# The conformer's LayerNorm placed inside the in-projection of a two-layer hybrid trunk

## The chip, the cores and the metric

One core of a Trainium2 chip runs the whole program. The metric is device time in microseconds (us) from one launch; lower is better. The core's engines work from queues of their own and meet through semaphores: TensorE (PE, with its weight loads PEld), VectorE (DVE), ScalarE (ACT), GpSimd (POOL) and SyncE (SP), which issues the loads.

## The reference, cut to what matters

Two layers, 512 tokens, width 1024, everything float32. In each layer one projection of the normed input feeds four mixers: A, a gated short convolution; B, a conformer convolution; C, a blockwise causal attention (MoBA, four heads of 64); D, a latent attention (MLA, four heads) whose query and key/value latents are normed by RMS. Their outputs are joined, projected, normed and added; a convolutional FFN follows. The change concerns mixer B:

```python
def conformer_conv_mixer(z, w_conv, b_conv, ln_g, ln_b):
    a, g = jnp.split(z, 2, axis=-1)
    u = a * jax.nn.sigmoid(g)
    u = causal_dwconv(u, w_conv) + b_conv.astype(u.dtype)
    return jax.nn.silu(layernorm(u, ln_g, ln_b))
```

`layernorm` takes the mean over the 256 channels of a token, subtracts it, divides by the root of the mean square (plus 1e-6), and applies a gain and a bias.

## The kernel before, in words

Activations lie transposed: channels on the 128 partitions, 512 tokens along the free axis. Every float32 product is made of three reduced-precision ones (`product`, lines 500 to 503): each operand is split in a high part, rounded by ScalarE ("hi"), and a low part, the rest, made by VectorE ("lo"); hi x hi, hi x lo and lo x hi are summed in one PSUM bank. Weights go the same way: SP loads a unit into `raw`, ScalarE writes its high part (line 400, `split_hi`), VectorE its low part (line 408, `split_lo`), in a ring of four.

The order of work is written out by hand, engine by engine. The in-projection is 21 groups, `for g in range(4, G_MK)` and `first_groups` on TensorE; a group is 24 products of 512 columns. Groups 0 to 3 feed the conformer, 4 to 9 MoBA, 10 to 14 the MLA latents (10 the key/value latent "ckv", 12 to 14 the query latents "cq"), 15 to 20 the gated convolution (gate, product, value; two halves). VectorE and ScalarE run the same loop `for g in range(G_MK)` with their work for each group. The conformer's 31 taps are spread over groups 3 to 14: one half of the channels is summed by VectorE in PSUM bank 7 (`CF_BANK`, lines 1074 and 1079), the other by ScalarE and POOL (lines 1373 and 824); both end in `cf_out`.

A norm over channels crosses partitions, so TensorE does it. There are three such events per layer, "ckv", "cq" and "ln", and each goes: ScalarE squares (`square`, line 1308, into `sq`), POOL adds the squares (`sums`, line 806), TensorE sums over partitions with a column of ones (`stat`, line 607, eight fp32 instructions into bank 4, `STAT`), VectorE makes the variance (`event_var`, line 952), POOL raises it to -1/2 (`rsqrt`, line 810, `rstd`), TensorE spreads it over the partitions (`spread`, line 614, eight fp32 instructions, again into `STAT`), VectorE multiplies. The LayerNorm also needs its mean, two fp32 products with a matrix of ones (line 659).

Before the change TensorE has: ckv's column sums after group 13, its spreading after group 15; cq's after 17 and 18; the LayerNorm's mean after group 19, into `STAT`; then the latent projections (keys `G_MK`, values `G_MV`, rope queries `G_MR`, queries `G_MQ`), with the LayerNorm's column sums between the two query groups; then the attention loop. POOL runs ckv, cq, the LayerNorm's sum, the rotation of the rope queries (lines 833 and 835), and then the LayerNorm's power.

The attention loop has 32 steps, one for a head (four MoBA, four MLA) and a chunk of 128 queries, with keys growing 128 to 512. A step: TensorE's `scores`; VectorE's masking and row maximum (line 1122) and, a step later, the reciprocal of the row sum (line 1130); ScalarE's exponential (line 1440); POOL's scaling (line 841, `prob`); three steps later TensorE's `transposes` (line 722), a head's four chunks taking one to four of them; ScalarE's high part (line 1432) and VectorE's low part (line 1136) of the transposed probabilities; then `values`. At step 2 POOL also makes the low part of the rope queries (line 845). The LayerNorm's second half hangs in these steps: TensorE's spreading at step 2, VectorE's products at 2 (line 1141), 5 and 6 (line 1146), 9 and 10 (line 1152), ScalarE's gain and tanh at 3 and 4 (lines 1445 and 1448) and high part at 6 and 7 (line 1452).

Banks are handed on through `bank_taken_over` and `bank_free`: a group waits until the last reader of its bank is done; so the second query group waits for the second gate's value product (line 1064), and the rope queries wait for the low parts of the three query latents (line 1085).

## Time and profile before

| | |
|---|---|
| three runs | 1259.45, 1260.35, 1263.19 us (median 1260.35) |
| the profiled execution | 1256.69 us, of it the span from first to last instruction 1254.6 us |
| TensorE busy | 1211.7 us, 97% of the span |
| VectorE, ScalarE, POOL busy | 820.4, 581.2, 208.8 us |
| mean granted clock of TensorE | 0.978 of full |

TensorE's busy time is modelled from pipelined instructions, and an instruction's duration reaches into the next one's start; so steps on TensorE are best read from start to start. The granted clock is 1.00 at 2.4 GHz and 0.50 at 1.2 GHz. A wait is put down to the semaphore that came last. The in-projection of layer 0 ends near 146 us of the span, its attention near 223.

### The profile page before, as it was taken

How to read it: one execution, taken by the hardware profiler on the slowest of the kernel's cores; microseconds unless marked ns; L12 is line 12 of the kernel's file. 1: busy time of each engine (PE TensorE's matmuls, PEld its weight loads, DVE VectorE, ACT ScalarE, POOL GpSimd, SP SyncE). 2: the span in 40 equal slices, each digit the busy share in tenths (PEclk: the TensorE clock that was granted, in tenths of full speed). 3: DMA queues.
4: the chain of work that ended last, by engine and by line, in shares of the span. 5: the costliest groups of instructions: out<-in, count | busy, mean ns of one | idle time of the engine just before them, and what ended most of it. 6: DMA issues, size and time to landing. Idle time of an engine off the chain costs nothing.

```text
span 1254.6 us, 15488 instructions
## 1 busy us (share of the span) xinstructions
PE 1211.7 (97%) x6006; PEld 1020.4 (81%) x6006; DVE 820.4 (65%) x1160; ACT 581.2 (46%) x879; POOL 208.8 (17%) x190
## 2 busy tenths in 40 slices
PE   6999999999999999999999999999999999999996
PEld 6887878888888888888888877788888888888885
DVE  4699557487666666544758976766766666664463
ACT  4455357454444344434545634755444444443432
POOL 1285136020000000000005822531000000000000
PEclk9999968999999999999999998899999999999998
DMA  8232312442333333466633333135233333336573
GB/s 241 80 85 82 88 43 84 148 138 85 101 101 101 96 90 100 146 190 216 202 85 98 84 94 86 33 133 169 85 113 90 100 101 91 94 101 199 171 231 121
DMA packets 157083, 147.36 MB, mean 117 GB/s; under 512 B 6831, under 2 KB 137811, under 8 KB 157011
## 3 DMA queue, kind: packets, MB, share of 16 engines
q1 hardware_dynamic: 156432, 145.64, 38.8%
q8 instruction: 48, 0.79, 0.3%
q10 hardware_dynamic: 579, 0.74, 0.2%
q14 instruction: 24, 0.20, 0.1%
HBM read 140.07 MB, written 2.10 MB: 113 GB/s over the span
## 4 chain that ended last, share of the span: by engine, by line
PE 82%; DVE 12%; POOL 2%; issue 2%; ACT 1%; DMA 1%; POOLq 0%; DVEq 0%; ACTq 0%
PE ps L501 26%; PE ps L503 26%; PE ps L502 26%; DVE ps L1074 3%; DVE wsp L408 3%; PE ps L722 2%; DVE rot L971 1%; PE ps L563 1%; POOL prob L841 1%; DVE shuf L969 1%; POOL rms_r L815 1%; DVE hid L976 1%; DVE xn L915 1%; DMA rows<-in_vectors 1%; POOL wsp L408 1%
## 5 line engine op out<-in xcount | busy, mean ns | idle before, releaser
L501 PE MATMUL ps<-xn,wsp 128*128 128x512 f32 (+2 forms) x1136 | 418.8, 369 | 11.4 <-DVE xn L915 11.4
L502 PE MATMUL ps<-xn,wsp 128*128 128x512 f32 (+2 forms) x1136 | 416.1, 366 | 0.0
L503 PE MATMUL ps<-xn,wsp 128*128 128x512 f32 (+2 forms) x1136 | 416.0, 366 | 0.0
L408 DVE TENSOR_TENSOR wsp<-raw,wsp 128x1024 fp32r<-128x1024 f32 (+1 forms) x250 | 311.1, 1247 | 155.5 <-ACT wsp L400 155.3
L400 ACT ACTIVATE wsp<-raw 128x1024 fp32r<-128x1024 f32 (+1 forms) x256 | 266.8, 1043 | 177.6 <-PE ps L503 146.5
L501 PEld LDWEIGHTS ps<-xn,wsp 128*128 128x128 f32 (+1 forms) x1136 | 215.1, 189 | 48.3 <-DVE xn L915 13.6
L502 PEld LDWEIGHTS ps<-xn,wsp 128*128 128x128 f32 (+1 forms) x1136 | 215.2, 189 | 35.0 <-issue 0.5
L503 PEld LDWEIGHTS ps<-xn,wsp 128*128 128x128 f32 (+1 forms) x1136 | 215.1, 189 | 34.9
L501 PE MATMUL ps<-wsp,hid 128*128 128x512 f32 (+1 forms) x488 | 189.7, 389 | 0.0
L503 PE MATMUL ps<-wsp,hid 128*128 128x512 f32 (+1 forms) x488 | 189.1, 388 | 0.0
L502 PE MATMUL ps<-wsp,hid 128*128 128x512 f32 (+1 forms) x488 | 189.0, 387 | 0.0
L815 POOL TENSOR_TENSOR rms_r<-rms_v,power 128x1 f32<-128x1 f32 x32 | 29.1, 913 | 833.9 <-DVE rms_v L880 833.9
L503 PEld LDWEIGHTS ps<-wsp,hid 128*128 128x128 f32 x488 | 91.6, 188 | 18.8
L502 PEld LDWEIGHTS ps<-wsp,hid 128*128 128x128 f32 x488 | 91.7, 188 | 18.6
L501 PEld LDWEIGHTS ps<-wsp,hid 128*128 128x128 f32 x488 | 91.7, 188 | 18.5
L824 POOL TENSOR_TENSOR cf_out<-cf_out,cf_tmp 128x512 f32<-128x512 f32 x60 | 94.4, 1573 | 71.1 <-ACT cf_tmp L1373 64.2
L1203 DVE SCALAR_TENSOR_TENSOR c_v<-ps,vec_all,c_v 128x511 f32<-128x511 f32 x44 | 33.0, 749 | 86.7 <-ACT c_v L1496 86.7
L1496 ACT ACTIVATE c_v<-ps,vec_all 128x512 f32<-128x512 f32 x44 | 30.3, 688 | 100.5 <-PE ps L503 100.5
L1203 DVE SCALAR_TENSOR_TENSOR c_g<-ps,vec_all,c_g 128x511 f32<-128x511 f32 x44 | 33.0, 750 | 62.7 <-ACT c_g L1496 62.7
L1496 ACT ACTIVATE c_g<-ps,vec_all 128x512 f32<-128x512 f32 x44 | 30.3, 688 | 76.6 <-PE ps L503 76.6
L1501 ACT ACTIVATE hid<-c_v 128x512 fp32r<-128x512 f32 x44 | 27.9, 633 | 62.0 <-DVE c_v L1225 62.0
L841 POOL TENSOR_TENSOR prob<-prob,rowinv 128x128 f32<-128x128 f32 (+1 forms) x64 | 45.6, 720 | 55.6 <-DVE rowinv L1130 55.4
(138 smaller groups left out, 1319.8 us busy)
## 6 DMA issues: line engine op xcount, KB each, us to landing
raw<-in_w_ffn_up SPq DMA_DIRECT2D x88, 512.0 KB, 3.8
raw<-in_w_ffn_down SPq DMA_DIRECT2D x88, 512.0 KB, 4.2
raw<-in_w_in SPq DMA_DIRECT2D x40, 512.0 KB, 3.9
raw<-in_w_out SPq DMA_DIRECT2D x32, 512.0 KB, 3.9
x<-in_x SPq DMA_DIRECT2D x4, 512.0 KB, 8.4
xn<-xn SPq DMA_DIRECT2D x8, 256.0 KB, 3.2
out_x<-x SPq DMA_DIRECT2D x4, 512.0 KB, 4.2
xn<-kr SPq DMA_DIRECT2D x8, 128.0 KB, 3.0
```

Source lines behind the costliest of these rows:

```text
L400: act.activation(wsp[:, u % SPLIT, 0, 0:nk * n], raw[:, r, 0:nk * n], ACT.Copy).then_inc(hi_done, 1)
L408: eng.tensor_tensor(wsp[:, u % SPLIT, 1, 0:nk * n], raw[:, (l * NU + u) % RAW, 0:nk * n], fp(wsp[:, u % SPLIT, 0, 0:nk * n]), ALU.subtract ...
L501: pe.matmul(dst, a[0], b[0], start=start, stop=False, skip_group_check=True)
L502: pe.matmul(dst, a[0], b[1], start=False, stop=False, skip_group_check=True)
L503: return pe.matmul(dst, a[1], b[0], start=False, stop=stop, skip_group_check=True)
L815: pool.tensor_tensor(rms_r[:, i:i + 1], rms_v[:, i:i + 1], power[:, 0:1], ALU.pow).then_inc(rms_rstd, 1)
L824: pool.tensor_tensor(cf_out[:, 1, :], cf_out[:, 1, :], cf_tmp[:, j % 2, :], ALU.add)\
L841: pool.tensor_tensor(prob[:, t % NPROB, 0:n], prob[:, t % NPROB, 0:n], rowinv[:, t:t + 1].to_broadcast([P, n]), ALU.mult).then_inc(prob_do ...
L1074: st.mark(dve.scalar_tensor_tensor(ps[:, CF_BANK, :], cf_u[:, 0, j:j + T], col(l, "conv_b", 2 * j), ps[:, CF_BANK, :], ALU.mult, ALU.add))
L1203: st.mark(dve.scalar_tensor_tensor(cc[:, 1:T], ps[:, bank, 0:T - 1], col(l, "conv_ffn", 2 * NF + half * NF + p), cc[:, 1:T], ALU.mult, ALU ...
L1496: act.activation((c_v if half else c_g)[:, :], ps[:, bank_of(G_UP + j), :], ACT.Copy, scale=col(l, "conv_ffn", 4 * NF + half * NF + p)).th ...
L1501: act.activation(hid[:, p, 0, :], c_v[:, :], ACT.Copy).then_inc(f_hi, 1)
```

## The change

The LayerNorm moves ahead as a whole. Its mean goes behind group 16, into bank 7, where VectorE's running sum of the taps has just ended, instead of bank 4; its column sums stand in the middle of group 18 and its spreading behind cq's after group 18, both in bank 7. It gets tiles of its own (`ln_sq`, `ln_var`, `ln_rstd`), so that it can run beside cq. ckv's spreading goes from after group 15 to after group 16, and VectorE's use of it from group 16 to 17. VectorE and ScalarE do the rest of the LayerNorm, with its gain, tanh and splitting, in groups 17 to 20; nothing of it is left in the attention steps. VectorE makes the low parts of the query latents in group 20, ahead of the second gate's value product, instead of after it. POOL's order becomes: power of ckv, sums of cq, sum of ln, power of cq, power of ln. The second value group, which uses bank 7, now waits for `cf_norm`. The scratch `sq`/`sm` moves by 96 bytes.

The diff, without the new tiles and the moves of those few bytes:

```diff
@@ -237,6 +240,10 @@
         ps = ctx.enter_context(nc.psum_tensor("ps", [P, 8, T], f32))
+        EV_BANK = dict(ckv=STAT, cq=STAT, ln=CF_BANK)
+        EV_SQ = dict(ckv=sq, cq=sq, ln=ln_sq)
+        EV_VAR = dict(ckv=var, cq=var, ln=ln_var)
+        EV_RSTD = dict(ckv=rstd, cq=rstd, ln=ln_rstd)
@@ -508,10 +515,10 @@
-def dense(u, bank, rhs, m=P, c0=0, cols=slice(0, T)):
+def dense(u, bank, rhs, m=P, c0=0, cols=slice(0, T), ks=None):
     w = weights(u)
     nk = len(rhs)
-    for k in range(nk):
+    for k in ks or range(nk):
         last = product(ps[0:m, bank, cols], (w[:, 0, k, c0:c0 + m], w[:, 1, k, c0:c0 + m]), rhs[k],
@@ -604,14 +611,14 @@
     for c in range(TC):
-        last = pe.matmul(ps[:, STAT, c:c + 1], sq[:, 0, c * P:(c + 1) * P], ones[:, 0:1],
+        last = pe.matmul(ps[:, EV_BANK[ev], c:c + 1], EV_SQ[ev][:, 0, c * P:(c + 1) * P], ones[:, 0:1],
                          start=True, stop=True)
...
     for c in range(TC):
-        last = pe.matmul(ps[:, STAT, c * P:(c + 1) * P], rstd[:, c:c + 1].to_broadcast([P, P]),
+        last = pe.matmul(ps[:, EV_BANK[ev], c * P:(c + 1) * P], EV_RSTD[ev][:, c:c + 1].to_broadcast([P, P]),
                          ident[:, :], start=True, stop=True)
@@ -641,23 +648,27 @@
             weights_ready(l, g)
-            last = dense(g, bank_of(g), x_pairs, m=MLA_QK if g == G_KR else P)
+            if g == 18:
+                dense(g, bank_of(g), x_pairs, ks=range(KD // 2))
+                stat("ln", l)
+                last = dense(g, bank_of(g), x_pairs, ks=range(KD // 2, KD))
+            else:
+                last = dense(g, bank_of(g), x_pairs, m=MLA_QK if g == G_KR else P)
         last.then_inc(group_done, 1)
...
             stat("ckv", l)
-        if g == 15:
+        if g == 16:
             spread("ckv", l)
+            pe.wait_ge(cf_conv, l + 1)
+            pe.wait_ge(cf_sum, (l + 1) * (CF_TAPS - 1))
+            for c in range(2):
+                last = pe.matmul(ps[:, CF_BANK, :], ones[:, :], cf_out[:, c, :], start=c == 0, stop=c == 1)
+            last.then_inc(mean_done, 1)
         if g == 17:
...
             spread("cq", l)
-        if g == 19:
-            pe.wait_ge(cf_conv, l + 1)
-            pe.wait_ge(cf_sum, (l + 1) * (CF_TAPS - 1))
-            pe.wait_ge(lat_norm, l * 4 + 4)
-            for c in range(2):
-                last = pe.matmul(ps[:, STAT, :], ones[:, :], cf_out[:, c, :], start=c == 0, stop=c == 1)
-            last.then_inc(mean_done, 1)
+            spread("ln", l)
@@ -669,6 +680,8 @@
         bank_taken_over(l, g)
+        if bank_of(g) == CF_BANK:
+            pe.wait_ge(cf_norm, l * 2 + 2)
         for j in range(2):
@@ -685,8 +698,6 @@
         dense(U_UQ, bank_of(g), latents, c0=i * P).then_inc(group_done, 1)
-        if i == 0:
-            stat("ln", l)
@@ -746,8 +757,6 @@
             scores(t)
-        if t == 2:
-            spread("ln", l)
         if TRAIL <= t < N_ATT + TRAIL:
@@ -756,7 +765,6 @@
     pe.wait_ge(y_ready, l * 4 + 4)
-    pe.wait_ge(cf_norm, l * 2 + 2)
     pe.wait_ge(masked, (l + 1) * N_ATT)
@@ -803,11 +811,12 @@
             pool.wait_ge(add_done, l * NADD + adds_before(ev) + k - 1)
-        pool.tensor_tensor(sq[:, 0, :], sq[:, 0, :], sq[:, 1, :], ALU.add).then_inc(add_done, 1)
+        tile = EV_SQ[ev]
+        pool.tensor_tensor(tile[:, 0, :], tile[:, 0, :], tile[:, 1, :], ALU.add).then_inc(add_done, 1)
...
     pool.wait_ge(var_done, l * NEV + EVENTS.index(ev) + 1)
-    pool.tensor_tensor(rstd[:, :], var[:, :], power[:, :], ALU.pow).then_inc(rstd_done, 1)
+    pool.tensor_tensor(EV_RSTD[ev][:, :], EV_VAR[ev][:, :], power[:, :], ALU.pow).then_inc(rstd_done, 1)
@@ -823,17 +832,17 @@
             .then_inc(cf_sum, 1)
-    for ev in ("ckv", "cq"):
-        sums(ev, l)
-        rsqrt(ev, l)
+    rsqrt("ckv", l)
+    sums("cq", l)
     sums("ln", l)
+    rsqrt("cq", l)
+    rsqrt("ln", l)
...
     pool.tensor_tensor(ml_rot[:, :], ml_rot[:, :], ml_shuf[:, :], ALU.add).then_inc(rot_done, 1)
-    rsqrt("ln", l)
@@ -949,7 +958,7 @@
     dve.wait_ge(stat_done, l * NEV + EVENTS.index(ev) + 1)
-    dve.tensor_scalar(var[:, :], ps[:, STAT, 0:TC], 1.0 / WIDTH[ev], EPS, ALU.mult, ALU.add)\
+    dve.tensor_scalar(EV_VAR[ev][:, :], ps[:, EV_BANK[ev], 0:TC], 1.0 / WIDTH[ev], EPS, ALU.mult, ALU.add)\
        .then_inc(var_done, 1)
@@ -976,7 +985,7 @@
     def group_a_lo(c):
-        dve.wait_ge(y_hi, l * 4 + c + 1)
+        dve.wait_ge(y_hi, l * 4 + 3 * c + 1)
         dst = hid[:, Y_SLOT["a"] + c]
@@ -999,7 +1008,7 @@
             event_var("ckv" if g == 14 else "cq", l)
-        if g == 16:
+        if g == 17:
             scale_ready("ckv", l)
@@ -1007,18 +1016,39 @@
                                      ALU.mult, ALU.subtract).then_inc(lat_ready, 1)
+        if g == 17:
+            dve.wait_ge(mean_done, l + 1)
+            for c in range(2):
+                dve.scalar_tensor_tensor(cf_out[:, c, :], ps[:, CF_BANK, :], -1.0 / GW, cf_out[:, c, :],
+                                         ALU.mult, ALU.add).then_inc(cf_cent, 1)
         if g == 18:
             group_a_lo(0)
+            event_var("ln", l)
         if g == 19:
...
                    .then_inc(lat_norm, 1)
+        if g == 19:
+            scale_ready("ln", l)
+            for c in range(2):
+                dve.tensor_tensor(cf_out[:, c, :], cf_out[:, c, :], ps[:, CF_BANK, :], ALU.mult)\
+                   .then_inc(cf_norm, 1)
+            for c in range(2):
+                dve.wait_ge(cf_swish, l * 2 + c + 1)
+                dve.scalar_tensor_tensor(cf_out[:, c, :], cf_th[:, c, :], 1.0, cf_out[:, c, :],
+                                         ALU.add, ALU.mult).then_inc(cf_val, 1)
         if g == 20:
-            dve.wait_ge(mean_done, l + 1)
+            for j in range(3):
+                dve.wait_ge(lat_hi, l * 4 + j + 2)
+                dst = hid[:, CQN + j]
+                dve.scalar_tensor_tensor(dst[:, 1, :], lat[:, j, :], col(l, "mla_q_norm", j),
+                                         fp(dst[:, 0, :]), ALU.mult, ALU.subtract).then_inc(lat_ready, 1)
             for c in range(2):
-                dve.scalar_tensor_tensor(cf_out[:, c, :], ps[:, STAT, :], -1.0 / GW, cf_out[:, c, :],
-                                         ALU.mult, ALU.add).then_inc(cf_cent, 1)
+                dve.wait_ge(y_hi, l * 4 + c + 2)
+                dst = hid[:, Y_SLOT["b"] + c]
+                dve.scalar_tensor_tensor(dst[:, 1, :], cf_out[:, c, :], 0.5, fp(dst[:, 0, :]),
+                                         ALU.mult, ALU.subtract).then_inc(y_ready, 1)
         if g in (1, 3):
@@ -1079,18 +1109,13 @@
     own(sc_val, l * 2 + 2)
-    for j in range(3):
-        dve.wait_ge(lat_hi, l * 4 + j + 2)
-        dst = hid[:, CQN + j]
-        dve.scalar_tensor_tensor(dst[:, 1, :], lat[:, j, :], col(l, "mla_q_norm", j),
-                                 fp(dst[:, 0, :]), ALU.mult, ALU.subtract).then_inc(lat_ready, 1)
     group_a_lo(1)
...
                           ALU.subtract).then_inc(kn_ready, 1)
-    own(y_ready, l * 4 + 2)
+    own(y_ready, l * 4 + 4)
     for half in range(2):
@@ -1105,8 +1130,6 @@
                           ALU.subtract).then_inc(qn_ready, 1)
-        if i == 0:
-            event_var("ln", l)
@@ -1135,22 +1158,6 @@
                .then_inc(pt_ready, 1)
-        if t == 2:
-            scale_ready("ln", l)
-            for c in range(2):
-                dve.tensor_tensor(cf_out[:, c, :], cf_out[:, c, :], ps[:, STAT, :], ALU.mult)\
-                   .then_inc(cf_norm, 1)
-        if t in (5, 6):
-            c = t - 5
-            dve.wait_ge(cf_swish, l * 2 + c + 1)
-            dve.scalar_tensor_tensor(cf_out[:, c, :], cf_th[:, c, :], 1.0, cf_out[:, c, :],
-                                     ALU.add, ALU.mult).then_inc(cf_val, 1)
-        if t in (9, 10):
-            c = t - 9
-            dve.wait_ge(y_hi, l * 4 + c + 3)
-            dst = hid[:, Y_SLOT["b"] + c]
-            dve.scalar_tensor_tensor(dst[:, 1, :], cf_out[:, c, :], 0.5, fp(dst[:, 0, :]),
-                                     ALU.mult, ALU.subtract).then_inc(y_ready, 1)
         h, r = divmod(t - TRAIL - VALUES_AFTER[2] - 2, TC)
@@ -1301,11 +1308,11 @@
     if k == 0:
-        if l or EVENTS.index(ev):
+        if ev != "ln" and (l or EVENTS.index(ev)):
             act.wait_ge(stat_done, l * NEV + EVENTS.index(ev))
...
         act.wait_ge(add_done, l * NADD + adds_before(ev) + k - 1)
-    act.activation(sq[:, min(k, 1), :], src, ACT.Square).then_inc(sq_done, 1)
+    act.activation(EV_SQ[ev][:, min(k, 1), :], src, ACT.Square).then_inc(sq_done, 1)
@@ -1391,28 +1398,39 @@
         if g == 17:
+            for c in range(2):
+                act.wait_ge(cf_cent, l * 2 + c + 1)
+                square("ln", c, cf_out[:, c, :], l)
             group_a_hi(0)
+        if g == 19:
+            for c in range(2):
+                act.wait_ge(cf_norm, l * 2 + c + 1)
+                act.activation(cf_out[:, c, :], cf_out[:, c, :], ACT.Identity,
+                               scale=col(l, "ln_b_gain", c), bias=col(l, "ln_b_bias", c))\
+                   .then_inc(cf_affine, 1)
+                act.wait_ge(cf_affine, l * 2 + c + 1)
+                act.activation(cf_th[:, c, :], cf_out[:, c, :], ACT.Tanh, scale=0.5).then_inc(cf_swish, 1)
         if g == 20:
...
                                scale=col(l, "mla_q_norm", j)).then_inc(lat_hi, 1)
+            for c in range(2):
+                act.wait_ge(cf_val, l * 2 + c + 1)
+                act.activation(hid[:, Y_SLOT["b"] + c, 0, :], cf_out[:, c, :], ACT.Copy, scale=0.5)\
+                   .then_inc(y_hi, 1)
         if g >= G_SC and (g - G_SC) % 3 == 0:
...
             act.activation(sc_w[:, :], ps[:, bank_of(g), :], ACT.Copy).then_inc(sc_gate, 1)
-        if g == 20:
-            for c in range(2):
-                act.wait_ge(cf_cent, l * 2 + c + 1)
-                square("ln", c, cf_out[:, c, :], l)
     group_a_hi(1)
...
         act.activation(ml_k[2 * i][:, 0, :], ps[:, bank_of(G_MK + i), :], ACT.Copy).then_inc(kn_hi, 1)
-    act.wait_ge(y_ready, l * 4 + 2)
+    act.wait_ge(y_ready, l * 4 + 4)
     for half in range(2):
@@ -1439,18 +1457,6 @@
                            scale=-1.0, accum_out=rowsum[:, t:t + 1]).then_inc(exp_done, 1)
-        if t in (3, 4):
-            c = t - 3
-            act.wait_ge(cf_norm, l * 2 + c + 1)
-            act.activation(cf_out[:, c, :], cf_out[:, c, :], ACT.Identity, scale=col(l, "ln_b_gain", c),
-                           bias=col(l, "ln_b_bias", c)).then_inc(cf_affine, 1)
-            act.wait_ge(cf_affine, l * 2 + c + 1)
-            act.activation(cf_th[:, c, :], cf_out[:, c, :], ACT.Tanh, scale=0.5).then_inc(cf_swish, 1)
-        if t in (6, 7):
-            c = t - 6
-            act.wait_ge(cf_val, l * 2 + c + 1)
-            act.activation(hid[:, Y_SLOT["b"] + c, 0, :], cf_out[:, c, :], ACT.Copy, scale=0.5)\
-               .then_inc(y_hi, 1)
         if t == 1:
...
         if t in (12, 16, 20):
```

## Rows read from the trace of the kernel before

**Rows 1.** The page: busy time, and the granted clock in 40 slices

```profile
PE 1211.7 (97%) x6006; PEld 1020.4 (81%) x6006; DVE 820.4 (65%) x1160; ACT 581.2 (46%) x879; POOL 208.8 (17%) x190
...
PEclk9999968999999999999999998899999999999998
```

**Rows 2.** Waits of TensorE: us in total, times, longest us

```profile
PE ps L614 <- POOL rstd L810: 3.0, 2, 1.5
```

**Rows 3.** Windows: us, busy of PE, PEld, DVE, ACT, POOL, clock, DMA share, GB/s

```profile
165.46:196.18 30.72, 30.72 (x118) 25.43 (x117) 16.30 (x55) 17.43 (x47) 10.32 (x13) 0.50 0.07 17
776.45:793.52 17.07, 17.07 (x60) 12.77 (x60) 9.48 (x34) 10.80 (x29) 7.11 (x10) 0.50 0.35 76
```

**Rows 4.** Timeline of TensorE after group 15: start us, us, what, idle before

```profile
114.23 1.16 PE L614 MATMUL ps<-ident,rstd 128*128 128x128 f32 x8 [1.48 <-POOL rstd L810]
```

**Rows 5.** Timeline of TensorE after groups 18 and 19, layer 0

```profile
132.52 1.05 PE L614 MATMUL ps<-ident,rstd 128*128 128x128 f32 x8
133.33 0.48 PE L501 MATMUL ps<-xn,wsp 128*128 128x512 f32 x1
...
138.89 1.88 PE L659 MATMUL ps<-cf_out,ones 128*128 128x512 f32 x4
```

**Rows 6.** Timeline of TensorE at the start of the rope queries, layer 0

```profile
148.64 0.28 PE L502 MATMUL ps<-wsp,hid 128*128 128x256 f32 x1
148.76 0.28 PE L503 MATMUL ps<-wsp,hid 128*128 128x256 f32 x1
149.15 0.50 PE L501 MATMUL ps<-hid,wsp 128*128 128x512 f32 x1
```

**Rows 7.** Timeline of TensorE at the entry into attention, layer 0

```profile
156.43 0.33 PE L501 MATMUL ps<-hid 64*128 64x128 f32 x1
...
158.12 0.44 PE L501 MATMUL ps<-hid 64*128 64x384 f32 x1 [0.74 <-DVE negmax L1122]
...
158.84 1.16 PE L614 MATMUL ps<-ident,rstd 128*128 128x128 f32 x8
159.92 0.49 PE L501 MATMUL ps<-hid 64*128 64x512 f32 x1
...
165.20 0.91 PE L722 MATMUL ps<-ident,prob 128*128 128x128 f32 x4 [0.98 <-POOL prob L841]
```

**Rows 8.** Timeline of TensorE at the entry into attention, layer 1

```profile
776.23 1.91 PE L614 MATMUL ps<-ident,rstd 128*128 128x128 f32 x8
778.07 0.79 PE L501 MATMUL ps<-hid 64*128 64x512 f32 x1
...
784.53 1.11 PE L722 MATMUL ps<-ident,prob 128*128 128x128 f32 x4
```

**Rows 9.** Timeline of TensorE, groups of four transposes of later heads, both layers

```profile
196.70 0.60 PE L722 MATMUL ps<-ident,prob 128*128 128x128 f32 x4
...
794.74 0.66 PE L722 MATMUL ps<-ident,prob 128*128 128x128 f32 x4
...
806.71 0.60 PE L722 MATMUL ps<-ident,prob 128*128 128x128 f32 x4
```

**Rows 10.** Timeline of POOL: the LayerNorm's sum and power, attention steps 2, 3

```profile
144.68 1.29 POOL L806 TENSOR_TENSOR sq<-sq 128x512 f32<-128x512 f32 x1 [14.12 <-ACT sq L1308]
...
156.08 1.02 POOL L810 TENSOR_TENSOR rstd<-var,power 128x4 f32<-128x4 f32 x1
...
162.86 1.28 POOL L845 TENSOR_TENSOR ml_rope<-ml_rot,ml_rope 128x512 fp32r<-128x512 f32 x1
164.09 1.06 POOL L841 TENSOR_TENSOR prob<-prob,rowinv 128x512 f32<-128x512 f32 x1
```

**Rows 11.** Timeline of VectorE: last tap, second gate, low parts of the query latents

```profile
114.56 0.75 DVE L1079 SCALAR_TENSOR_TENSOR cf_out<-cf_u,vec_all,ps 128x512 f32<-128x512 f32 x1
...
139.08 0.69 DVE L1052 TENSOR_TENSOR sc_u<-ps,sc_w 128x512 f32<-128x512 f32 x1 [2.91 <-PE ps L503]
...
147.01 2.08 DVE L1085 SCALAR_TENSOR_TENSOR hid<-lat,vec_all,hid 128x512 fp32r<-128x512 f32 x3
```

More of the change, by code:

```diff
@@ L182, in hybrid_trunk_kernel @@
         rstd = place("rstd", [P, TC], f32)
+        ln_var = place("ln_var", [P, TC], f32)
+        ln_rstd = place("ln_rstd", [P, TC], f32)
         power = place("power", [P, TC], f32)
@@ L193, in hybrid_trunk_kernel @@
         sc_u = place("sc_u", [P, T + 2], f32, tmp_at + 4096)
-        sq = place("sq", [P, 2, T], f32, tmp_at + 10336)
-        sm = place("sm", [P, 2, T], f32, tmp_at + 10336)
+        sq = place("sq", [P, 2, T], f32, tmp_at + 10240)
+        sm = place("sm", [P, 2, T], f32, tmp_at + 10240)
         prob = place("prob", [P, NPROB, T], f32, tmp_at + 4096)
@@ L202, in hybrid_trunk_kernel @@
         junk = place("junk", [P, D], bf16, tmp_at + 12288, width=2)
-        assert tmp_at + 14432 <= nc.sbuf_usable_end, (tmp_at + 14432, nc.sbuf_usable_end)
+        assert tmp_at + 14336 <= nc.sbuf_usable_end, (tmp_at + 14336, nc.sbuf_usable_end)
         Y_SLOT = dict(a=0, b=2, c=4, d=6)
@@ L229, in hybrid_trunk_kernel @@
         ml_shuf = place("ml_shuf", [P, T], f32, slot(Y_SLOT["d"]) + 4 * T)
+        ln_sq = place("ln_sq", [P, 2, T], f32, slot(Y_SLOT["d"] + 1))
         ml_rope = place("ml_rope", [P, 2, T], f32r, slot(Y_SLOT["d"] + 1))
```

## The prediction

> **What bounds the kernel now.** I read the page first: TensorE is busy 97% of the span [rows 1], so what counts is its work, its idle time and its clock; another engine matters only where TensorE waits for it. The list of TensorE's waits then says which of them this change can reach [rows 2]: 3.0 us, twice 1.5, behind POOL's rsqrt `rstd` at line 810 (the ckv norm of each layer). The rest of what it can reach is read from the timelines around its places. The clock is the third thing. The windows give its two low stretches [rows 3]: 30.72 us in layer 0 and 17.07 us in layer 1 at 0.50 (1.2 GHz), and the page's clock line shows every other slice up to the last at nine tenths or more (1.00, 2.4 GHz) [rows 1]. Both begin a few us after attention begins and end inside it.
>
> The cost of the low level is read from the groups of four transposes that close a head's steps [rows 7 to 9]. In layer 0 three heads, from 165.20 to 196.70, took 31.50 us; in layer 1 two heads at the full level, from 794.74 to 806.71, took 11.97, which is 5.99 a head. So layer 0 lost about 31.50 - 3 x 5.99 = 13.5 us, and layer 1 in its one slow head (784.53 to 794.74, 10.21 us) 4.2 us and a little before that.
>
> **The change, part by part.** Most of what moves costs TensorE the same wherever it stands: the eight column sums of `stat("ln")` and the four products of the mean keep their kind and count. What differs:
>
> 1. *The ckv spreading goes from after group 15 to after group 16.* Its `rstd` came 1.48 us after TensorE was ready [rows 4]; now a whole group of 24 products lies between, and DVE's last tap of the running sum, which the mean waits for, ends at 115.3 [rows 11], also before group 16 can end. The wait goes: -1.48 per layer, -2.96.
>
> 2. *The wait before the rope queries goes.* `dense(U_UR)` started 0.39 us after the product ahead of it [rows 6], where products of that shape follow at 0.12, because the three low parts of the q latents were made at 147.01 for 2.08 us [rows 11], behind the second gate's product. They now stand ahead of that product. The wait goes: -0.27 per layer, -0.54. Late next is the second gate itself, which the second query group's bank waits for. DVE had 2.91 us idle ahead of group 19's gate [rows 11]; it now puts four LayerNorm operations there, whose two last ones follow ScalarE's tanh. Counted on, the gate's product ends some 3 us before TensorE asks for its bank: cost 0, or up to +1 per layer if ScalarE's turns are slower.
>
> 3. *The ln spreading is now behind the cq spreading, between groups 18 and 19.* Eight fp32 products took 0.81 us there, 132.52 to 133.33 [rows 5]: +0.81 per layer, +1.62. Its `rstd` has the second half of group 18, the column sums and the cq spreading as cover. POOL's power itself takes 1.02 [rows 10], with the variance on DVE ahead of it. If that cover failed it would cost up to +1 per layer; I take 0.
>
> 4. *The column sums in the middle of group 18* wait for POOL's sum of squares. From the mean's start, 138.89 [rows 5], to the end of that sum, 144.68 + 1.29 [rows 10], it took 7.1 us. Now the mean, group 17, the cq sums and half of group 18 lie between, by the same spacing about 10.5 us. Cost 0, with 3 us to spare. On POOL the sum now stands ahead of `rsqrt("cq")`, which is wanted only after group 18.
>
> 5. *The entry into attention.* In layer 0 the first score started at 156.43 and the first four transposes at 165.20 [rows 7], 8.77 us. The 0.74 us wait for the first mask stays: it hangs on the second query group's low part, which nothing here brings nearer. The spreading's 1.08 us (158.84 to 159.92) goes, and with it the two LayerNorm products on DVE that held back the fourth mask. But the fourth `prob` also stood behind POOL's rope subtraction [rows 10], which stays. Replaying the chain, the four transposes come about 1.2 us earlier, with a wait of about 0.9 still ahead of them. That holds if the clock stays up so long. If it falls at the fourth score, the entry takes what layer 1's took from there, 784.53 - 778.07 = 6.46 us [rows 8], and comes at 8.96 us: +0.2. I take the middle, -0.5. In layer 1 the spreading itself ran at the low level, 776.23 to 778.07 [rows 8]: 1.84 us go and the rest is as before, -1.74 after 0.1 for the restart. If the clock there holds longer, up to -3.1.
>
> 6. *DVE's and ScalarE's LayerNorm operations in steps 2 to 10 go.* TensorE was busy throughout the low stretches [rows 3], so that relief buys nothing there: 0.
>
> Sum: -2.96 - 0.54 + 1.62 - 0.5 - 1.74 = **-4.1 us**. The profiled execution took 1256.69 us (span 1254.6), so it would take 1252.6. But the three runs shown stand at 1259.45 to 1263.19, their median 1260.35 lying 3.66 above the profiled one. I read that as low stretches of other lengths, an estimate: layer 1's alone would have lost 9 us more had it lasted as long as layer 0's. I take the sum off the median: **1256.2 us**.
>
> **Where a rule and the rows part.** Before both falls TensorE did short scores, transposes and waits of at most 0.98 us [rows 7]; in layer 1 the fall came at 776.45, within the eight spreading products [rows 3, 8], in layer 0 only 6.6 us after they had begun. So the plain products of the spreading did not keep the clock up in layer 1 and may have delayed the fall in layer 0; that is the choice made in step 5. The Trainium skill, "TensorE: Matmul & The Clock Gate", section "Part 4: PE-mode transpose", says that transposes do not count as a busy TensorE in the way other products do. By that rule the change speaks against itself, since it takes eight plain products out of a stretch that holds transposes; layer 0's entry would then be the +0.2 of step 5 and the sum -3.4.
>
> **The rivals.**
>
> *The gain is eaten by a longer low stretch.* For it: layer 0 shows that the stretch can last until the MLA heads, layer 1 that it can end two heads sooner, and nothing in the change sets which. If layer 1's lasts like layer 0's it loses 13.5 - 4.2 = 9.3 us more than in the profile: 1252.6 + 9.3 = 1261.9. With only one more slow head in either layer, 4.5 us: 1257.1 on the profile's base, 1259 to 1260 on the median's. Against it: the runs shown probably hold such stretches already. Chance 0.24, result 1257 to 1262, no change.
>
> *The clock does not fall in one layer.* For it: the entry is shorter by a spreading. Against it: the 0.74 us wait, the half-height scores and the POOL wait all stay, and TensorE has less work between them. It would save 4 to 13.5 us more: about 1247. Chance 0.08.
>
> *DVE becomes the bound around groups 19 to 21.* For it: seven operations more there, about 5 us with the turns to ScalarE, and the second gate, the key and value low parts and the first mask queue behind them on DVE. It decides once DVE ends its chain later than ScalarE ends the second query group's high part; from there each us on DVE is one us of TensorE, in both layers. Against it: DVE's idle stretches there [rows 11]. One us late in both gives 1256.2 + 2 = 1258.2. Chance 0.10.
>
> *Slower: the low level reaches into the MLA heads.* There the full level held in both layers once it had come back [rows 1, 3]. If the shifted schedule makes it stay low through the four MLA heads of one layer, that is 4 x (10.5 - 5.99) = 18 us (10.5 is a third of layer 0's 31.50): 1256.2 + 18 = 1274; a single such head, with the longer stretch above, 1265. Against it: the rise in layer 0 came just there, at 196.18. It decides where the low stretch outlasts the first MLA head, within which it ended in layer 0. Chance 0.08.
>
> *The change doesn't do what it says.* It does: every instruction of `ln` leaves the attention loop; no chance of its own.
>
> **How the numbers follow.** The forecast has 0.50; its own range is 1253.5 to 1258.5, from step 5's ends and the +1 of steps 2 and 3. Steps of 0.3% (3.8 us, about what a measurement of this kernel can tell from no change) stand at 1256.6 and 1264.1. The forecast is so near the first that about 0.42 of its 0.50 lies below it. Faster: 0.42 + 0.08 = 0.50. Same: 0.08 + 0.24 + 0.10 = 0.42. Slower: 0.08. The range for 8 in 10 leaves out the slower case, and the better part of the missing fall: 1250.5 to 1262.
>
> **What would show it.** In the changed profile: the wait of TensorE on `rstd` gone from the list of waits; the three latents' wait gone; two spreadings back to back after group 18; the first score of layer 0 about 0.9 us earlier; the four transposes 7.5 to 9 us after it; the fourth `prob` still waiting behind the rope subtraction; two low stretches of the clock, each beginning in the entry. Wrong would be: a TensorE wait in the middle of group 18 or ahead of group 19, a first mask later than 1.35 us after the first score, or low stretches whose total differs from 47.8 us by so much that the 4 us drown in it.

## The result: 8.7 us faster, 3.3 us below the range

| | before | after |
|---|---|---|
| median of the runs compared | 1255.92 us (20 runs, 1246.69 to 1263.19) | 1247.20 us (20 runs, from 1244.45) |
| ratio | | 0.995, 95% interval 0.9927 to 0.9973 |
| profiled execution, its span | 1256.69, 1254.6 us | 1257.87, 1256.1 us |

The prediction said 1256.2 us (1250.5 to 1262.0). The 8.7 us are the difference of the medians; by the means of the same runs (1254.8 and 1249.0) it is 5.8. One disturbed execution of the changed kernel, 6798.82 us, takes no part in the ratio. Two things stand out. The kernel before, with 17 more runs, has a median of 1255.92, not the 1260.35 of the three runs shown ahead of the prediction. And the profiled execution of the changed kernel was one of its longest, so its total misleads; it has to be read stage by stage.

The page of the changed kernel, busy time and granted clock:

```profile
PE 1217.1 (97%) x6006; PEld 1026.6 (82%) x6006; DVE 822.8 (66%) x1160; ACT 581.7 (46%) x879; POOL 208.7 (17%) x190
...
PEclk9999959999999999999999998699999999999999
```

The instruction counts are those of [rows 1]: nothing was added or left out. From the list of TensorE's waits (us in total, times, longest us), the two that stand in the attention's entry and heads:

```profile
PE ps L733 <- POOL prob L850: 3.6, 8, 0.6
PE ps L508 <- DVE negmax L1145: 1.5, 2, 0.7
```

The 3.0 us behind `rstd` [rows 2] are gone; the wait for the first mask stayed, twice 0.7. TensorE's timeline of layer 0: the two spreadings after group 18, the start of the rope queries, the first and third score, the first transposes, the first group of four. After the dots, the first score and the first group of four of layer 1.

```profile
132.53 1.05 PE L621 MATMUL ps<-ident,rstd 128*128 128x128 f32 x8
133.42 1.06 PE L621 MATMUL ps<-ident,ln_rstd 128*128 128x128 f32 x8
...
147.90 0.28 PE L510 MATMUL ps<-wsp,hid 128*128 128x256 f32 x1
148.02 0.40 PE L508 MATMUL ps<-hid,wsp 128*128 128x512 f32 x1
...
154.26 0.32 PE L508 MATMUL ps<-hid 64*128 64x128 f32 x1
...
155.95 0.44 PE L508 MATMUL ps<-hid 64*128 64x384 f32 x1 [0.73 <-DVE negmax L1145]
...
157.37 0.33 PE L733 MATMUL ps<-ident,prob 128*128 128x128 f32 x1
...
161.56 1.12 PE L733 MATMUL ps<-ident,prob 128*128 128x128 f32 x4
...
769.59 0.32 PE L508 MATMUL ps<-hid 64*128 64x128 f32 x1
...
777.08 1.11 PE L733 MATMUL ps<-ident,prob 128*128 128x128 f32 x4
```

The first score of layer 1 in the kernel before:

```profile
773.83 0.33 PE L501 MATMUL ps<-hid 64*128 64x128 f32 x1
```

The rope queries start 0.12 us after the product ahead of them, where it was 0.39 [rows 6]. From the first score to the first four transposes it is 7.30 us, where it was 8.77 [rows 7], and the 0.98 us wait ahead of them is gone too. In layer 1 it is 7.49 us (769.59 to 777.08), where it was 10.70 (773.83 to the 784.53 of [rows 8]). What hides this in the total is the clock. The windows of its low stretches, layers 0 and 1 (columns as in [rows 3]):

```profile
159.39:193.52 34.13, 34.04 (x126) 27.91 (x127) 15.15 (x55) 16.45 (x46) 13.21 (x16) 0.50 0.11 23
773.79:807.92 34.13, 34.13 (x128) 27.59 (x126) 15.40 (x59) 17.16 (x47) 13.02 (x16) 0.50 0.13 28
```

In layer 1 the stretch was twice as long as in [rows 3], and it ran, as there, with TensorE busy all through.

Stage by stage, all from starts in TensorE's timeline (us). The 80 transposes of an attention are counted here in fours, in the order in which they are issued: "first", "third", "fourth" and "fifth" are the starts of numbers 1, 9, 13 and 17. These fours are not the groups of four that close a head: the first head's group is numbers 7 to 10, the second head's begins with number 17.

| stage | before, layers 0 / 1 | after, layers 0 / 1 |
|---|---|---|
| program start to ckv's column sums, layer 0 | 100.76 | 99.73 |
| ckv's column sums to the first score | 55.68 / 55.71 | 54.53 / 54.54 |
| first score to first | 4.38 / 5.81 | 3.11 / 3.10 |
| first to fourth | 9.47 / 10.17 | 9.50 / 9.68 |
| fourth to the last transposes | 48.97 / 40.03 | 49.30 / 48.76 |

From the column sums to the fourth the change gained 2.39 us in layer 0 and 4.37 in layer 1, **6.76 us** in all (7.00 up to the first head's group of four, the mark that the prediction used), where the prediction's sum had 4.1. The longer low stretch took 8.73 back in the last row of layer 1. The first row differs by 1.03 us for work that the change does not touch; in a second profile of the changed kernel it was 100.76 again.

### The profile page after: what moved, and what is told of

It reads as the page before. It is cut to its first block, busy times and chain, and to the rows that moved or that the text cites. A ratio compares the mean times of both kernels' runs of the same rounds, so it can differ in the third digit from the quotient of the medians.

```text
span 1256.1 us, 15486 instructions
## 1 busy us (share of the span) xinstructions
PE 1217.1 (97%) x6006; PEld 1026.6 (82%) x6006; DVE 822.8 (66%) x1160; ACT 581.7 (46%) x879; POOL 208.7 (17%) x190
## 4 chain that ended last, share of the span: by engine, by line
PE 88%; DVE 4%; POOL 4%; issue 1%; ACT 1%; DMA 1%; POOLq 0%; DVEq 0%; ACTq 0%
PE ps L508 28%; PE ps L510 28%; PE ps L509 28%; PE ps L733 2%; POOL cf_out L833 2%; POOL rms_r L824 1%; POOL prob L850 1%; PE ps L570 1%; DVE xn L924 1%; DMA rows<-in_vectors 1%; DVE wsp L415 1%; DVE yt L904 1%; PE ps L621 0%; PE ps L614 0%; DVE sm L1145 0%
```

## The experiments

They ask two questions. Is the gain work and waits (theory A at first: about 4 us of these, and shorter low stretches for the rest; theory B: work and waits alone; theory C: a wait replaced by another)? And where in the kernel does it lie? Four kernels came first, two of them with the clock held up by idle products.

**The ckv spreading alone.** The kernel before, with one part of the change:

```diff
-                    if g == 15:
+                    if g == 16:
                         spread("ckv", l)
-                    if g == 16:
+                    if g == 17:
                         scale_ready("ckv", l)
```

> The kernel before with one part of the change alone: ckv's spreading after group 16 instead of 15, and VectorE's use of it in group 17. Theory A (the gain is a fixed part of about 4 us, waits that are gone, and on top of it the low stretches of the clock come out shorter): the list of TensorE's waits has no wait on rstd any more, and at an equal granted clock a run is 3.0 us shorter than before (1.48 a layer); the low stretches are as long as before's. Theory B (the whole difference of the medians, 8.7 us, is work and waits, and the clock has no part in it): this part, the largest wait removed, would carry at least 4 us. Theory C (neither wait mattered, something later takes their place): no change.

1255.1 us (12 runs, 1241.83 to 1260.68) against 1255.17; ratio 0.9967 (0.9932 to 1.0002). The total tells nothing: its runs spread over 19 us with the clock. The trace tells more: in layer 1, column sums to first score took 54.02 us, where before took 55.71, so the part is worth **1.69 us** there. (Layer 0 has a low stretch of 3.41 us at 102.36 in this stage and can't be compared.) The wait on `rstd` is gone from TensorE's list; a new one, for ScalarE's squares, stands ahead of the column sums, 0.91 us in each layer. It lies before the stage, and in layer 0 before everything that the edit moves.

**The spreading put back.** The kernel after, with eight idle products of the spreading's kind at step 2:

```diff
+                    if t == 2:
+                        pe.wait_ge(vl_ready, l * 2 + 2)
+                        for c in range(TC):
+                            pe.matmul(ps[:, CF_BANK, c * P:(c + 1) * P], ln_rstd[:, c:c + 1].to_broadcast([P, P]),
+                                      ident[:, :], start=True, stop=True)
```

> The kernel after, with eight fp32 spreading products put back at step 2 of the attention loop as idle work (they write bank 7, which nobody reads). Theory A, with the spreading in the entry as a cause of longer low stretches: the runs go back to before's spread, a median 4 to 8 us above after's, the mean granted clock 0.975 to 0.978 instead of 0.982. If instead the spreading does not steer the clock: only its own time, 1.1 to 1.8 us a layer where TensorE had no idle time to hide it, 1 to 3.6 us in all. Theory B: 2 to 3.6 us, the clock as in after.

1249.03 us (8 runs); ratio 0.9931 (0.9907 to 0.9955). That lies between the 1247.2 and the 1250.3 (below) of the kernel after itself and decides nothing either. Its mean clock, 0.982 over the eight runs, is not below the 0.978 of the kernel after in the first comparison, so theory A's longer low stretches from a spreading in the entry were not seen. In its layer 1 first score to first took 4.39 us at the full clock, where the kernel after took 3.10 and the kernel before, in layer 0, 4.38.

**The clock held up.** Both kernels, with twelve idle products a layer on bank 7 in steps 2 to 6:

```diff
+                def filler(n):
+                    for _ in range(n):
+                        pe.matmul(ps[:, CF_BANK, :], hid[:, KM, 0, 0:P], hid[:, KM, 0, :], start=True, stop=True,
+                                  skip_group_check=True)
+
+                FILL = {2: 3, 3: 1, 4: 2, 5: 2, 6: 4}
...
+                    if t == 2:
+                        pe.wait_ge(vl_ready, l * 2 + 2)
+                        filler(FILL[2])
                     if t < N_ATT:
                         scores(t)
+                    if 2 < t < N_ATT:
+                        filler(FILL.get(t, 0))
```

> The kernel after, with twelve idle products of 512 columns a layer in attention steps 2 to 6, placed where TensorE waits (three ahead of the third score, the others ahead of the transposes of steps 3 to 6); they write bank 7, which nobody reads. Theory A: if the low stretches come from the sparse entry, the clock stays at 1.00 through attention in both layers or nearly, the mean granted clock rises above 0.99, and the runs come to 1232 to 1239 us with little spread (after's 1247 less 10 to 15). Theory B: the fillers that are not hidden cost up to 12 x 0.23 x 2 = 5.5 us and nothing is gained.

> The kernel before with the same twelve idle products a layer. Theory A: the low stretches go here too, and what is left between this run and the filled kernel after is the fixed part of the change alone, 4 to 5 us (2.96 + 0.54 - 1.62 for the waits and the moved spreading, and 1 to 1.2 a layer for the shorter entry). Theory B: the filled pair differs by the same 8.7 us as the unfilled one.

After: **1234.53 us** (5 runs, 1233.15 to 1235.15), ratio 0.982 (0.9796 to 0.9844). Before: 1242.05 us (6 runs, 1240.88 to 1252.86), ratio 0.9901 (0.9866 to 0.9937). Both profiles have a mean clock of 0.997 and no low stretch in attention; of the filled before's six runs one, the longest, had 0.988. So the medians of the pair differ by 7.5 us with the clock nearly out of play, nearly as much as without fillers; theory A's 4 to 5 us is too small. The clock line of the filled kernel after:

```profile
PEclk9999999999999999999999999999999999999998
```

The list of TensorE's waits of the filled kernel after, the line on the probabilities:

```profile
PE ps L733 <- POOL prob L861: 4.5, 8, 0.7
```

The same list of the filled kernel before, which has four such waits more and two lines that the other lacks:

```profile
PE ps L722 <- POOL prob L852: 5.6, 12, 0.7
PE ps L614 <- POOL rstd L821: 3.0, 2, 1.5
PE ps L607 <- ACT sq L1319: 0.5, 1, 0.5
```

Held so, the stages repeat to 0.02 us in both layers, and the difference can be laid out. "Third to fifth" is, as counted above, from number 9 of an attention's transposes, in the first head's group of four, to number 17, the start of the second head's:

| stage, us a layer | filled before | filled after | difference |
|---|---|---|---|
| ckv's column sums to the first score | 55.75 | 54.51 | -1.24 |
| first score to first | 4.81 | 3.52 | -1.29 |
| third to fifth | 6.84 | 6.06 | -0.78 |

Twice -3.31 is -6.6 of the 7.5 us; of the rest, 0.5 is the wait at L607 above, which stands ahead of the column sums of layer 1. In the third row stand the four waits that the filled kernel after lacks, two in each layer. Layer 0 of the filled kernel before, from the first head's group of four to the second's, 7.06 us:

```profile
164.79 0.60 PE L722 MATMUL ps<-ident,prob 128*128 128x128 f32 x4
...
167.88 0.44 PE L722 MATMUL ps<-ident,prob 128*128 128x128 f32 x2 [0.22 <-POOL prob L852]
...
170.02 0.55 PE L722 MATMUL ps<-ident,prob 128*128 128x128 f32 x3 [0.36 <-POOL prob L852]
...
171.85 0.66 PE L722 MATMUL ps<-ident,prob 128*128 128x128 f32 x4
```

The same two groups in the filled kernel after, 6.27 us apart:

```profile
162.06 0.60 PE L733 MATMUL ps<-ident,prob 128*128 128x128 f32 x4
...
168.33 0.66 PE L733 MATMUL ps<-ident,prob 128*128 128x128 f32 x4
```

The next kernels take these rows one at a time, with fillers to hold the clock. In their expectations theory D is that all 7.5 us are removed work and waits, E that a removed wait comes back elsewhere.

**Row 1: the ckv spreading**, moved as above, in the filled kernel before.

> The kernel before with the twelve filler products a layer, and with the ckv spreading one group later. Theory D (the whole difference of the filled pair, 7.5 us, is work and waits that the change removes, about 3.5 to 4 a layer): the ckv wait of 1.5 us goes in each layer and nothing takes its place, so 1242.05 - 3.0 = 1239.0 us. Rival E (the ckv wait comes back elsewhere, at the mean or at the next bank, and the pair differs by something else): 1241 to 1242 us. Both expect a granted clock of 0.996 or more.

1240.02 us (4 runs, 1238.73 to 1241.41), 2.0 below the filled before's median, and 1.0 short of the 3.0 expected, which the medians of a few runs can't settle. The trace can. From the column sums to the first score of layer 1, here and then in the filled kernel before:

```profile
708.71 1.05 PE L607 MATMUL ps<-ones,sq 128*128 128x1 f32 x8 [0.54 <-ACT sq L1319]
...
762.72 0.33 PE L501 MATMUL ps<-hid 64*128 64x128 f32 x1
```

```profile
706.49 1.05 PE L607 MATMUL ps<-ones,sq 128*128 128x1 f32 x8 [0.50 <-ACT sq L1319]
...
762.24 0.33 PE L501 MATMUL ps<-hid 64*128 64x128 f32 x1
```

That is 54.02 us against 55.75, -1.73 (layer 0 holds a low stretch of 3.41 us at 103.88 and can't be compared). In layer 0 the wait for the squares was 0.91 us, where the filled before had none; as in the first of these kernels it stands before everything that the edit moves, and it takes back a part of the gain in the total. Of the -1.24 in the first row, then, -1.73 are the ckv part, and +0.49 the rest: the ln spreading that came in (+0.9) and the rope queries' wait that went (-0.26), with small restarts.

**Row 2: the spreading in the entry**, put back idle in the filled kernel after (the edit of the spreading put back, behind the fillers).

> The kernel after with the fillers, and with eight idle spreading products back at step 2. Theory D: they cost their own 1.1 to 1.2 us in each layer, since TensorE waits for no mask there once the fillers stand in it: 1236.8 us. Rival E (they hide in the waits for the mask and for POOL, as step 5 took most of layer 0's to do): 1234.5 to 1235.3 us.

1238.29 us (4 runs, 1236.78 to 1238.45); 2.3 were expected, 3.8 came in the medians. The stage carries 2.6 of these; the profile has besides a low stretch of 3.41 us at 862.77, outside the attention. First score to first took 4.81 us in both layers, exactly the filled before's. Its timeline:

```profile
154.10 0.32 PE L508 MATMUL ps<-hid 64*128 64x128 f32 x1
...
156.59 1.16 PE L771 MATMUL ps<-ident,ln_rstd 128*128 128x128 f32 x8
...
158.91 0.27 PE L733 MATMUL ps<-ident,prob 128*128 128x128 f32 x1
```

So the spreading costs its whole length (156.59 to 157.68, where the next score starts) and slower starts around it, 1.29 us in each layer; none of it hides.

**Row 3: the LayerNorm's operations in the attention steps.** First VectorE's alone, then ScalarE's alone, as idle operations of the same size into a dead tile (the edits shortened; VectorE's are six, two of them at step 2; the text below counts them as eight):

```diff
+                    if t == 2:
+                        for c in range(2):
+                            dve.tensor_tensor(cf_out[:, c, :], causal[:, 0:T], causal[:, 0:T], ALU.mult)
+                    if t in (5, 6, 9, 10):
+                        dve.scalar_tensor_tensor(cf_out[:, (t - 5) % 4, :], causal[:, 0:T], 1.0, causal[:, 0:T],
+                                                 ALU.add, ALU.mult)
```

```diff
+                    if t in (3, 4):
+                        act.activation(cf_out[:, t - 3, :], causal[:, 0:T], ACT.Identity, scale=gain, bias=bias)
+                        act.activation(cf_out[:, t - 3, :], causal[:, 0:T], ACT.Tanh, scale=0.5)
+                    if t in (6, 7):
+                        act.activation(cf_out[:, t - 6, :], causal[:, 0:T], ACT.Copy, scale=0.5)
```

> The kernel after with the fillers, and with the eight LayerNorm operations that the change took from DVE's attention steps put back there as idle ones of the same size (two at step 2, one each at steps 5, 6, 9 and 10; they write a dead tile). Step 6 of the prediction priced them at 0: then 1234.5 us. Theory D: at the full clock they hold up the masks and so the probabilities of the second head, 0.8 to 1.0 us a layer, and the two at step 2 up to 0.5 more: 1236 to 1237.5 us, with TensorE waiting on POOL's probabilities at the second head again.

> The kernel after with the fillers, and with the six LayerNorm operations that the change took from ScalarE's attention steps put back there as idle ones (Identity and Tanh at steps 3 and 4, Copy at steps 6 and 7, into a dead tile). In the filled kernel before, ScalarE's first pair stood from 161.54 to 162.91 us ahead of the second head's copies and exponentials, and TensorE then lost 0.79 us a layer between the third and the fifth group of four transposes. Theory D with ScalarE as the cause: that 0.8 comes back in each layer, 1234.5 + 1.6 = 1236.1 us, with waits on POOL's probabilities in the second head. Rival (step 6 of the prediction, or it takes both engines' operations together): 1234.5 to 1235 us.

VectorE's: 1234.66 us (4 runs); third to fifth stayed at 6.05, and 0.53 us a layer came in elsewhere, a wait for the fourth mask behind the two operations of step 2:

```profile
159.79 0.38 PE L508 MATMUL ps<-hid 64*128 64x256 f32 x1 [0.45 <-DVE negmax L1156]
```

ScalarE's: 1234.29 us (4 runs), every stage as in the filled kernel after. Both theories that named one engine fell. Then both together, with the waits between them (ScalarE's first operation waits for VectorE's product, an operation of VectorE for ScalarE's tanh, ScalarE's copy for that):

> The kernel after with the twelve fillers, and with the LayerNorm operations of both engines put back in the attention steps as idle ones, with the waits between them as before: ScalarE's Identity and Tanh wait for DVE's two products of step 2, DVE's operations of steps 5 and 6 for the Tanh, ScalarE's Copies of steps 6 and 7 for those. Alone, neither engine's brought back the 0.79 us a layer between the third and the fifth group of four transposes. Theory D' (the turns between the two engines make it): those two steps take 3.04 and 3.80 us in place of 2.75 and 3.31, and with the 0.53 that DVE's two products of step 2 cost, 1234.5 + 2 x 0.79 to 2 x 1.32 = 1236.1 to 1237.1 us. Rival (it also needs the spreading, which brings TensorE to the second head later): 2.75 and 3.31 us, 1234.5 to 1235.6 us.

Third to fifth took 3.76 + 3.82 = 7.58 us in layer 0, and the two waits are back to the hundredth, with another for a mask ahead of them:

```profile
166.05 0.33 PE L508 MATMUL ps<-hid 64*128 64x128 f32 x1 [0.67 <-DVE negmax L1156]
...
166.81 0.44 PE L733 MATMUL ps<-ident,prob 128*128 128x128 f32 x2 [0.22 <-POOL prob L861]
...
168.95 0.55 PE L733 MATMUL ps<-ident,prob 128*128 128x128 f32 x3 [0.36 <-POOL prob L861]
```

So the operations of both engines together, with the waits between them, hold up the second head's masks and probabilities. It is more than was to be explained: 1.52 us against the 0.78 of the table, with a wait of 0.67 us that the filled kernel before lacks. That the turns do it, and not the load of both engines, is argued and not shown: no kernel had both engines' operations without the waits between them. The time missed what both sides expected, 1247.90 us (10 runs, 1241.81 to 1257.79): with these operations twelve fillers no longer held the clock. The window in layer 1:

```profile
773.47:797.36 23.89, 23.86 (x92) 19.94 (x92) 12.12 (x45) 13.73 (x36) 9.03 (x11) 0.50 0.00 1
```

**The clock's share.** The kernel after once more, beside before on one chip, 12 and 17 runs.

> The kernel after once more, unchanged, beside the kernel before on one chip. Theory D (work and waits alone): its runs have the same mean granted clock as the kernel before's (0.978 to 0.980), and stand about 7 us below them. Rival A (part of the gain is shorter low stretches): its mean granted clock is 0.002 to 0.004 higher than the kernel before's, and at an equal clock it stands only 4 us below.

1250.31 us (1244.46 to 1258.62) against 1255.22; ratio 0.9961 (0.9932 to 0.9991). Each run's time follows its mean granted clock:

| granted clock of the run | before, us | after, us |
|---|---|---|
| 0.982, 0.983 | 1252.03 to 1253.61 (6 runs) | 1244.46, 1244.70 |
| 0.978, 0.979 | 1252.54 to 1257.52 (5) | 1248.79, 1250.28, 1250.34 |
| 0.974 to 0.977 | 1257.99 to 1258.62 (3) | 1251.91 to 1253.85 (3) |
| mean over all runs | 0.9789 (17) | 0.9768 (12) |

At one clock the kernel after stands 5.5 to 8.5 us lower (medians of the rows; the runs at other clocks, three of before and four of after, have no counterpart), and its mean clock is no higher. A straight line of time against clock, through all 62 runs of the kernel before beside the experiments and the 31 of the kernel after, puts the kernel after 7.1 us lower at an equal clock. Rival A falls: the change does not shorten the low stretches. Theory D's 7 us stand at an equal clock only; the medians differ by 4.9. The low stretches vary from run to run, and move a median of 12 to 20 runs by some 2 us either way (8.7 us in the first comparison, 4.9 in this one); the means, 5.8 and 5.1, agree better.

**Fewer fillers**, in the kernel after; the change against its twelve:

```diff
-                FILL = {2: 3, 3: 1, 4: 2, 5: 2, 6: 4}
+                FILL = {2: 3, 4: 1, 5: 1, 6: 2}
```

> The kernel after with seven fillers a layer in place of twelve (three at step 2, one each at steps 4 and 5, two at step 6). Five fewer cost 5 x 0.23 = 1.15 us less in each layer, of which some only fill a wait. If the clock holds: 1232.3 to 1233.5 us with a granted clock of 0.996 or more. If it falls in one layer: 1236 to 1243 us at 0.985 to 0.992.

> The kernel after with four fillers a layer (three at step 2, one at step 6). If the clock holds: 1231 to 1232.5 us at 0.996 or more. If it falls in one layer: 1236 to 1243 us; in both: 1245 to 1250 us, as the kernel after without fillers.

Seven (the diff): **1232.19 us** (4 runs, 1231.98 to 1232.94), ratio 0.9799 (0.9758 to 0.984), the fastest kernel here; the profile's mean clock is 0.996. Four (three at step 2, one at step 6): 1249.02 us (10 runs, 1240.1 to 1257.88); the profile shows the fall in layer 1 alone, and by their mean clocks of 0.970 to 0.990 the other runs differ in how much of it they had:

```profile
763.23:783.71 20.48, 19.98 (x73) 15.87 (x73) 8.42 (x33) 8.77 (x25) 6.36 (x9) 0.50 0.12 27
```

## Why the prediction was wrong, step by step

It missed by 9.0 us: 4.4 from the base, 4.6 from the sum. Of the 4.6, the stages show 2.9 (7.0 gained against 4.1); the rest is scatter of the medians.

- **The base failed.** The prediction put it so: "I take the sum off the median". Three runs at 1259.45 to 1263.19 were the upper end of a spread of 16 us. Their median lay 4.43 above that of 20 runs, 1255.92, which the profiled execution (1256.69) was near. Off the profiled execution the same sum gives 1252.6.
- **Step 1 held**, and was 0.2 us a layer too small: 1.69 to 1.73 measured, 1.48 predicted. The wait is listed with 1.48 [rows 4], but the spreading stood 1.64 later than a product in its place would have (112.36 to 114.23, less 0.23).
- **Steps 2, 3 and 4 held**: together +0.49 us a layer measured (54.51 against 54.02), -0.27 + 0.81 = +0.54 predicted. No wait appeared in the middle of group 18 or ahead of group 19.
- **Step 5 failed**, and it is the larger part of the sum's miss: "I take the middle, -0.5" in layer 0, "-1.74" in layer 1. Measured from the first score to the first group of four: -1.47 (8.77 to 7.30) and -3.21 (10.70 to 7.49). The replay of the chain had given 1.2 for layer 0 and the upper end 3.1 for layer 1. Both were near; I took the one back for an earlier fall of the clock, and for the other kept the fall where it had been. In layer 1 the clock did hold longer, the condition of the 3.1 (below). In layer 0 the clock did fall earlier, 5.1 us after the first score (154.26 to 159.39) where before it was 9.0 [rows 3, 7], but the group of four came 4.19 us after the first transposes (157.37 to 161.56), no later than before (4.38): at the low level TensorE was busy until its probabilities were there. The 0.9 us wait that I said would stay did not; in the kernel with four fillers, whose layer 0 kept the full clock, it stood with 0.54 us, and the group of four came 7.39 us after the first score. So the early fall took nothing back there.
- **Step 6 failed where the clock was held**: "0". In the profiles without fillers the third-to-fifth stretch lies in a low stretch and gains nothing, as predicted. Where the clock is held it is 0.78 us a layer, and neither engine alone makes it.
- **The rule weighed against the trace.** The Trainium skill, "TensorE: Matmul & The Clock Gate", section "Part 4: PE-mode transpose", says that transposes do not count as busy in the way other products do. By it, eight plain products fewer would bring the low level sooner. In layer 0 the fall came sooner after the first score, by 3.9 us, and seven plain products more held the full level; both agree with it. In layer 1 it came later, 4.2 us after the first score (769.59 to 773.79) where before it was 2.6 (773.83 to the 776.45 of [rows 3]), so the rows do not settle it, and the loss that the prediction took from the rule was not there. Nor do the five profiles without fillers: the fall came 9.0, 2.6, 7.6, 6.9, 3.3 and 6.9 us after the first score where a spreading stands in the entry, and 5.1, 4.2, 3.5 and 4.2 where none does.
- **The rivals.** The longer low stretch was in the profiled execution (8.73 us in layer 1) but not in the mean; the missing fall was not seen in either profile; VectorE as the bound around groups 19 to 21 and the low level in all MLA heads did not come. They priced the clock as one pattern for the changed kernel; the runs show that one kernel has many. In the first rival the time with one more slow head on the median's base should be 1260.7 by its own terms, 1256.2 + 4.5, and not 1259 to 1260; it changes no chance.

The 6.8 to 7.0 us of the two profiles, the 6.6 of the held pair's stages and the 7.1 us at equal clock agree; what the first comparison has beyond them, some 2 us of its 8.7, is the scatter that the second shows on the other side. What makes a low stretch end sooner in one run than in another was not found.

## What to carry to other kernels

Where a run's time follows its granted clock, compare stages of two traces and not totals, and take the base from many runs, not from three and not from one profiled execution (here 0.8 us above the median before the change and 10.7 above it after). Replay the chain of waits and keep its result; an allowance for the clock belongs in the range. If the clock falls in a stage of short products, try a few idle products to hold it: seven a layer were worth more here than the change (15 us against 8.7), and the runs so held, all but one, lie within 1 to 4 us of each other. How many it takes has to be tried out: four were too few here, and twelve too few once more waits stood in the stage.

## What was unexpected of the hardware

In layer 1 of the changed kernel's profile the clock stayed at 0.50 for 34.13 us in which TensorE was busy for all 34.13, with waits of at most 0.73 us in the entry ahead of it; seven idle products of 0.23 us a layer in steps 2 to 6 kept it at 0.996 over the whole run; four did so in layer 0 alone of the one profile. And the stretches differ in length from run to run: five profiles without fillers show 10.24 to 37.55 us in a layer, for attention steps that are the same but for the LayerNorm.
